# Prompt memory's products, the state space squares' sums and three groups of loads take other places in the mixers of a two-layer decoder step

## The reference

```
x = x + W_o [ MLA(8 heads) | Mamba-2 SSD(4 heads) | GLA(4 heads) ](rmsnorm(x))
x = x + MemCrossAttn(rmsnorm(x), memory K/V)      (4 heads over 256 memory tokens)
x = x + ConvGatedMLP(rmsnorm(x))
```

## Time and profile before

| | us |
|---|---|
| median of 3 runs (1399.82 to 1403.01) | 1400.36 |
| the profiled execution | 1399.61 |
| its span in the trace | 1397.8 |
| PE busy | 1363.8 |
| DVE busy | 893.5 |
| ACT busy | 594.6 |
| POOL busy | 206.8 |

### The profile page before, as it was taken

The page is one execution under the profiler, slowest core; times in us unless marked ns, Lnnn a source line. Parts: engine busy times, 40 slices in busy tenths (PEclk is TensorE's granted clock), DMA queues, the critical chain, the costliest instruction groups (busy, mean ns, idle before and its releaser), DMA issues.

```text
span 1397.8 us, 23318 instructions
## 1 busy us (share of the span) xinstructions
PE 1363.8 (98%) x8148; PEld 1122.8 (80%) x8148; DVE 893.5 (64%) x1850; ACT 594.6 (43%) x1607; POOL 206.8 (15%) x330
## 2 busy tenths in 40 slices
PE   9999899999999999999999999999999999999999
PEld 6676757777776999999977677677777669999999
DVE  1337558888425877896423665688882358788963
ACT  2166657767325333320012766577761343333200
POOL 1001022211012122220000101212200121222200
PEclk9999899999999999999999997999999999999999
DMA  7331434443044434444433323444431354444442
GB/s 276 111 117 66 165 115 122 121 114 104 3 161 174 135 124 149 132 139 136 152 130 115 107 98 118 124 132 113 122 79 31 136 187 131 142 138 135 138 138 87
DMA packets 79718, 175.24 MB, mean 125 GB/s; under 512 B 11793, under 2 KB 46130, under 8 KB 78706
## 3 DMA queue, kind: packets, MB, share of 16 engines
q1 hardware_dynamic: 75952, 164.11, 36.7%
q0 software_dynamic: 3360, 9.18, 2.2%
q10 hardware_dynamic: 290, 0.45, 0.1%
HBM read 167.42 MB, written 6.29 MB: 124 GB/s over the span
## 4 chain that ended last, share of the span: by engine, by line
PE 61%; DVE 24%; ACT 9%; issue 3%; DMA 1%; SPq 1%; DVEq 0%
PE pair L517 13%; PE pair L877 8%; DVE area L1685 8%; PE pair L1159 8%; PE pair L878 8%; ACT area L1881 4%; PE pair L994 3%; PE bank L1159 3%; PE bank L913 2%; DVE area L1703 2%; DVE area L1709 2%; PE pair L884 2%; ACT area L1887 2%; PE pair L969 2%; DVE area L1701 2%
## 5 line engine op out<-in xcount | busy, mean ns | idle before, releaser
L517 PE MATMUL pair<-xg,slot 128*128 128x320 f32 x768 | 211.9, 433 | 1.9 <-DMA slot<-in_weights 1.9
L1554 DVE TENSOR_REDUCE small<-sq 128x8 f32<-128x512 f32 x256 | 168.0, 681 | 50.4 <-ACT sq L2120 49.2
L517 PEld LDWEIGHTS pair<-xg,slot 128*128 128x128 f32 x768 | 144.9, 190 | 64.5 <-issue 3.2
L2120 ACT ACTIVATE sq<-pair 128x512 f32<-128x512 f32 x256 | 152.2, 595 | 5.7 <-DVE small L1554 5.7
L1685 DVE TENSOR_TENSOR area<-slot 128x512 f32<-128x512 f32 (+1 forms) x128 | 85.2, 667 | 42.7 <-PE pair L1159 42.7
L1128 PE MATMUL pair<-sq,area 128*128 128x160 f32 x736 | 112.0, 301 | 0.1
L877 PE MATMUL pair<-wkq,area 128*128 128x288 f32 x320 | 107.6, 418 | 0.0
L1128 PEld LDWEIGHTS pair<-sq,area 128*128 128x128 f32 x736 | 102.8, 190 | 1.8 <-DVE area L1685 1.2
L878 PE MATMUL pair<-wkq,area 128*128 128x288 f32 x320 | 103.8, 406 | 0.0
L1881 ACT ACTIVATE area<-area 128x336 f32<-128x336 f32 (+6 forms) x114 | 62.2, 549 | 94.4 <-DVE area L1703 79.8
L2325 POOL DMA_INDIRECT krT<-in_cache_r,kr_rows x64 | 61.6, 963 | 226.7 <-PE pair L884 224.0
(11 more groups left out here) (458 smaller groups left out, 2685.4 us busy)
## 6 DMA issues: line engine op xcount, KB each, us to landing
slot<-in_weights SPq DMA_DIRECT2D x216, 512.0 KB, 3.9
area<-in_cache SPq DMA_DIRECT2D x160, 130.0 KB, 2.1
kept<-in_cache SPq DMA_DIRECT2D x96, 130.0 KB, 2.2
slot<-in_weights SPq DMA_DIRECT2D x18, 384.0 KB, 3.3
xg<-in_ssd_t SPq DMA_DIRECT2D x2, 1024.0 KB, 4.8
area<-in_ssd_n SPq DMA_DIRECT2D x2, 1024.0 KB, 10.8
hs_out<-area POOLq DMA_DIRECT2D x2, 1024.0 KB
x<-in_x SPq DMA_DIRECT2D x4, 320.0 KB, 6.0
```

The costliest lines, as they stand in the source:

```text
L517: last = mm(out[:, 0:T], w[:, k, :], xg[:, k, :], start=(k == 0), stop=(k == KD - 1))
L1554: dve.tensor_reduce(ssk[:, t % 2, 8 * j:8 * j + 8], ksq[k % 3], AX.X, ALU.add).then_inc(V.fire(on["k_summed"]), 1)
L2120: f(ksq[k % 3].rearrange("p (a h) d -> p a h d", a=2), b4[:, :, :, NQ - at:NQ - at + 64], ACT.Square).then_inc(A.fire(on["key_free"]), 1)
```

## The change

- TensorE, attention: part 1 of the memory products in quarters of two steps at h = 1 to 4; nothing at h = 5 and 6; part 4 still at h = 7; the first two quarters of part 2 at h = 8 and 9.
- TensorE, later: the third and fourth quarter of part 2 ahead of the SSD token tiles 2 and 3; the first half of part 3 between the two `yi` tiles and the second half behind them.
- ScalarE: part 1's copies at h = 5, part 4's logarithm and exponential at h = 8, part 2's copy after the token tiles, part 3's copy between the exponential of `gek` and `own_samples`.
- `ssd_norm` goes from ahead of `gla` on TensorE to behind `o` 4, in front of the samples' GLA states; ScalarE's two logarithms and exponential for it go from behind the squares of y to behind the squares of o; VectorE's `ssd_out` goes behind the last samples' states. The squares of o are written to `sq[:, 2:4]`, so that y's stay in `sq[:, 0:2]`.
- SP: the seven weight loads go behind the samples' states, GLA's states and the first two page groups.

```diff
@@ TensorE, prompt_attention
-                    if 1 <= h <= 6:
-                        memory_keys(l, (h + 1) // 2, range(0, 4) if h % 2 else range(4, KD))
+                    if 1 <= h <= 4:
+                        memory_keys(l, 1, quarter(h - 1))
                     if h == 7:
                         memory_keys(l, 4)
+                    if h in (8, 9):
+                        memory_keys(l, 2, quarter(h - 8))
...
+            def quarter(i):
+                return range(2 * i, 2 * i + 2)
@@ TensorE, tokens_first
                 for f in range(4):
+                    if f >= 2:
+                        memory_keys(l, 2, quarter(f))
@@ TensorE, ssd, ahead of each yi and behind both
+                    if g:
+                        memory_keys(l, 3, range(0, 4))
...
+                memory_keys(l, 3, range(4, KD))
@@ TensorE, gla
                 last.then_inc(banks.full("o", l, 4), 1)
+                ssd_norm(l)
                 pe.wait_ge(*on["vm_ready"].at(l))
@@ TensorE, gla_norm
-                    mm(b[:, 0:T], cc("blk64"), sq[:, g, :], **F)...
+                    mm(b[:, 0:T], cc("blk64"), sq[:, 2 + g, :], **F)...
@@ TensorE, main loop
                 gla_inputs(l)
-                ssd_norm(l)
                 gla(l)
@@ VectorE, gla
-                ssd_out(l)
...
                 states(l, 1, 1)
+                ssd_out(l)
@@ ScalarE, prompt_attention
-                    if h in (2, 4, 6, 7):
-                        memory_keys(l, (h + 1) // 2)
+                    if h == 5:
+                        memory_keys(l, 1)
+                    if h == 8:
+                        memory_keys(l, 4)
@@ ScalarE, ssd
                 for k in range(4):
                     token_tile(l, k)
+                memory_keys(l, 2)
                 gla_decay(l)
...
                 exp(gek, gek, scale=1.0 / 16).then_inc(A.fire(on["gek_ready"]), 1)
+                memory_keys(l, 3)
                 own_samples(l, bm, 256, "bm_ready")
...
                 f(sq[:, 0:2, :], ysb, ACT.Square).then_inc(A.fire(on["y_sq"]), 1)
-                (for both tiles: wait for y_ss, ln; then exp, y_rs)
@@ ScalarE, gla
-                f(sq[:, 0:2, :], osb, ACT.Square).then_inc(A.fire(on["o_sq"]), 1)
+                f(sq[:, 2:4, :], osb, ACT.Square).then_inc(A.fire(on["o_sq"]), 1)
+                (for both tiles: wait for y_ss, ln; then exp, y_rs)
@@ SP
                 sp.dma_start(hT_t, io["ssd_t"][l]).then_inc(hT_in, 16)
-                limit[:] = [filled[0] + NSLOT]
-                fill(("wuv", "wo"))
-                limit.clear()
...
                 for t in range(2):
                     group(l, t)
+                limit[:] = [filled[0] + NSLOT]
+                fill(("wuv", "wo"))
+                limit.clear()
```

More of the change, by code:

```diff
@@ L857, in gla_norm @@
                     pe.wait_ge(*banks.before("o_ss", l, g))
-                    mm(b[:, 0:T], cc("blk64"), sq[:, g, :], **F).then_inc(banks.full("o_ss", l, g), 1)
+                    mm(b[:, 0:T], cc("blk64"), sq[:, 2 + g, :], **F).then_inc(banks.full("o_ss", l, g), 1)
             def cache_group(l, t):
@@ L2065, in ssd @@
                 f(sq[:, 0:2, :], ysb, ACT.Square).then_inc(A.fire(on["y_sq"]), 1)
[L2066 to L2071, removed]
             def gla_decay(l):
@@ L2094, in gla @@
                 act.wait_ge(*A.last)
-                f(sq[:, 0:2, :], osb, ACT.Square).then_inc(A.fire(on["o_sq"]), 1)
+                f(sq[:, 2:4, :], osb, ACT.Square).then_inc(A.fire(on["o_sq"]), 1)
+                for g in range(2):
+                    b = banks.of("y_ss", l, g)
+                    act.wait_ge(*banks.filled("y_ss", l, g))
+                    ln(ytmp[:, g, :], b[:, 0:T], 128).then_inc(A.free("y_ss", l, g), 1)
+                act.wait_ge(*A.last)
+                exp(ytmp, ytmp, scale=-0.5).then_inc(A.fire(on["y_rs"]), 1)
                 for g in range(2):
```

## The result

The changed kernel takes 1416.97 us (median of 4 runs, 1415.25 to 1422.58) against 1400.09 for the kernel before in the same runs (1399.37 to 1403.01). The ratio is 1.013, with a 95% interval of 1.0109 to 1.0150: slower by 1.3%. I had forecast 1403.0 with a range of 1395 to 1412, so the direction was the likeliest of the three and the size is outside the range. What happened is the rival "low clock until the cache", and it is dearer than I made it.

What follows compares the result with a forecast made beforehand. It took the chain of waits leaving the mixers through VectorE's `mix_gla` as the bound: -2.3 us over both layers at full clock plus 5.0 for low clock made +2.7, 1402.3 profiled, 1403.0 as median; range 1395 to 1412.

Steps and rivals of the forecast that it cites:

- low clock until the cache: Rival: clock already low when `gla` starts and low up to the cache, 7 us a layer, +11.7, 1412 us; chance 0.17.
- ScalarE held by part 3's copy: In the SSD, ScalarE idles from about 165 to 170.8, so `gla` starts at 179.1 in layer 0, 869.7 in layer 1.
- The first dips gone: Low clock at 156.9 and 846.4, behind the wait ahead of token tile 3, disappears: 1.6 us in layer 0, 3.3 in layer 1.
- The dip behind `yi`: y, the transposes and `a`, 7.6 us in layer 0 mostly at low clock, were estimated at 4 us at full clock.
- The attention's 0.5 us: Part 1's squares and copy leave ScalarE's path ahead of head 3: 0.5 us gained, last head's copy at 149.9.
- The norm: `ssd_norm`'s squares' sums moved behind `o` 4: cost 1.3 us a layer, between 0 and 2; nothing gained ahead of `gla`.
- The loads: 3.6 MB of weights wait for part 3 and end by 181: cost 0, up to 2 us if still under way at `mix_gla`.
- the low-clock term of the sum: Low stretch of 6.6 us at the wait ahead of `gla`, 1.7 inside it, half the other 4.9: 2.5 us a layer.
- the second rival: The rival "low clock until the cache", listed second after the rival that the clock stays up through `gla`; chance 0.17.

Runs made afterwards that it cites:

- the two pairs with and without it: Norm's products, logarithms and `ssd_out` back at their old places: on the changed kernel, ratio 1.0113 against 1.0130; on the kernel with the queue freed, 0.9980 against 0.9976.
- the queue freed: Changed kernel with one line moved, ScalarE's copy of part 3 behind `gla_keys` instead of ahead of `own_samples`: 1394.77 us, ratio 0.9976 to the kernel before.
- the wait filled: Changed kernel with four extra products per layer that nothing reads, in TensorE's wait for `gla_keys` ahead of `gla`: 1395.25 us, ratio 0.9969 to the kernel before.
- part 3 left out: Kernel with the queue freed, part 3 moved from `yi` to ahead of the cache's third page group, weight loads behind the twelfth: 1397.99 us, ratio 0.9997.
- part 1 in halves: Kernel with the queue freed, part 1 of the memory products in halves at h = 1 and 2 of the attention: 1395.70 us, ratio 0.9971.

## Why the prediction was wrong

- *ScalarE held by part 3's copy: right.* Idle 6.44 us (4 to 6 predicted); the copy at 171.43 (170.8 predicted), `gla` at 179.62 and 880.85 less 10.4 inherited, 870.4 (179.1 and 869.7), behind a wait of 3.75 (4).
- *The first dips gone: right*, and by the mechanism I named, the filled wait ahead of tile 3. The dip behind `yi` went too (864.9 to 877.0 at 1.00, before 0.50 from 859.9), which I had only half counted on.
- *The attention's 0.5 us: not there.* The last copy is at 150.37 (149.9 predicted, 150.40 before). Part 4's logarithm and exponential, 0.68 and 0.63 us at 147.64, stand ahead of the last head; that they give back what part 1's squares had freed is my reading and was not run by itself.
- *The norm: wrong as the price of the move, +1.3 us a layer against nothing*, shown by the two pairs with and without it. I took the sums at their old place for free because ScalarE starts `gla`; but they need the squares of y, which ScalarE makes behind `gla_keys`, so there they add 2.5 us ahead of `gla` (182.08 against 179.62). The 15.3 us from the start of `gla` to the end of `mix_gla` were right at full clock: 175.93 to 191.28 with the queue freed, 181.38 to 196.72 with the wait filled.
- *The loads: right as a term* (no wait on them anywhere), but I missed that their move was needed at all: +47 us without it.
- *The step that failed is the low-clock term of the sum.* I had seen the wait, its releaser and that a shorter one was followed by a low clock, and then sized the stretch by a typical length, 6.6 us, and its cost at 2.5 a layer. It lasted 20.1 and 23.3 us. From the first product of `gla` to the end of `mix_gla` the sum had 15.3 + 2.5 = 17.8 us in each layer; measured were 24.5 in layer 0 and 25.0 in layer 1. That is 13.9 us missing, and the profiled execution is 13.2 above the sum's 1402.3. Against the 15.3 at full clock the low clock costs 9.2 and 9.7 a layer, where I had 2.5.

The trace held what was needed to choose right. In the earlier trace rows the clock stayed low over 10.2 us of `yi`, y and `a` with TensorE busy throughout. I named that under the second rival and gave it 0.17. By its own rule (11.9 us of TensorE to L858 "doubled") this rival would have been 11.9 a layer, and I cut it to 7 as "nearer to the middle". Uncut it gives -2.3 + 23.8, 1421, nearer to the 1415.5 measured than my forecast was. The Trainium skill ("TensorE: Matmul & The Clock Gate", "HAM oscillation") says that a loop whose matmuls take less time than the wait for the next data loses the clock in every pass. This trace agrees on the loss and goes further, since with one wait of 3.75 us the clock was low for 20.1 us of busy TensorE.

## What to carry to other kernels

Read the granted clock of each stretch beside TensorE's busy share: a wait of a few microseconds ahead of narrow matmuls can cost far more than its own length. Here 3.75 us of wait made 15.3 us of work into 24.5 and 25.0. Fill such a wait with dense products, useful or not (two of them a layer were worth 3.5 us here, four some 22), or move what causes it. Compare the same work and not the same microseconds in two traces, and more than one trace before a short dip is put down to an edit. And before an operation is put into a queue in the middle of a stage, list what stands behind it: a copy of 0.38 us at the head of ScalarE's queue cost 1.5% of the kernel.

## What the runs showed of the hardware

- TensorE stayed at the low clock through 20.1 and 23.3 us without a pause, over products of 16, 64 and 128 columns, of 32 rows by 512 columns, and also over the squares' sums of 128 rows by 320 columns (L788, from 192.85 to 195.3 in layer 0). It was at full clock again 0.4 us behind the start of the cache's first 288-column scores in layer 0 (200.61, 1.00 from 201.0) and 1.8 us behind it in layer 1 (902.34, 0.94 in 904.1 to 904.4).
- The length of the wait alone does not decide whether the clock falls. In the kernel with the freed queue the wait for the third page group was 2.69 us in layer 0 and 2.62 in layer 1; the first was followed by 6.7 us at 0.50, and behind the second the clock stayed at 1.00. The fall behind `yi` with part 3 left out came after 7.0 us of which TensorE was busy for 6.76, and the one in GLA with part 1 in halves after 17.7 us of which it was busy for 17.61.
- Four products of 128x512 in f32 that nothing reads, 3.70 us, kept the clock up through all 12 us of GLA behind them, in both layers; the kernel's ten runs had mean granted clocks of 0.996 to 1.000, the changed kernel's four 0.976 to 0.982.
